# A two-layer hybrid trunk: the decay step ahead of a rotation, a joint opened on 256 columns, a table load moved behind a split, whole tiles two units later

## What is computed

```python
h   = rmsnorm(x) * (1 + scale1) + shift1
# one projection of h in parts: u, q, k, v, z, xbc, dt
A   = pooling_mixer(u)                    # windows 2/4/8/16
B   = differential_attention(q, k, v)     # rotary on the latent q, k; 4 heads
C   = ssd_mixer(conv(xbc), dt, z)         # chunked scan, both directions
x  += gate1 * (out_proj(sum of sigmoid(gates(h)) * branch_proj(A, B, C)))
x  += gate2 * conv_ffn(rmsnorm(x) * (1 + scale2) + shift2)
```

## Time and profile before

| what | value |
|---|---|
| runs | 1292.47, 1293.12, 1292.94 us; median 1292.94 |
| profiled execution | 1292.74 us |
| its span in the profile | 1290.9 us, so 1.84 us lie around it |
| TensorE's granted clock | 0.998 of full speed |
| PE busy | 1272.4 us |
| DVE busy | 1084.3 us |
| ACT busy | 651.0 us |
| POOL busy | 196.6 us |

### The profile page before, as it was taken

How to read it: one execution, slowest core, us unless ns; L and a number is a source line. 1 busy time by engine, 2 the same in 40 slices (tenths; PEclk the granted TensorE clock), 3 DMA queues, 4 the chain that set the end, 5 groups by cost and what they waited for, 6 DMA issues and landing times.

```text
span 1290.9 us, 20336 instructions
## 1 busy us (share of the span) xinstructions
PE 1272.4 (99%) x7704; PEld 1227.6 (95%) x7704; DVE 1084.3 (84%) x1996; ACT 651.0 (50%) x1098; POOL 196.6 (15%) x191
## 2 busy tenths in 40 slices
PE   7999999999999999999999999999999999999997
PEld 5999899999999999999999988999999999999997
DVE  6899978788988999999969998877988799999433
ACT  5633555655565554443374336654455754544432
POOL 0269100002200000001104950000040000000110
PEclk9999999999999999999999999999999999999999
DMA  9566446444533454457735662564445354544441
GB/s 362 201 229 212 148 139 218 167 148 131 164 130 131 133 170 155 147 191 273 234 120 168 227 210 84 178 230 149 137 126 194 93 168 132 166 139 161 152 127 57
DMA packets 60482, 216.26 MB, mean 168 GB/s; under 512 B 7105, under 2 KB 9409, under 8 KB 58849
## 3 DMA queue, kind: packets, MB, share of 16 engines
q1 hardware_dynamic: 56224, 199.38, 46.1%
q0 software_dynamic: 4016, 15.39, 3.8%
q10 hardware_dynamic: 144, 0.20, 0.0%
HBM read 211.17 MB, written 3.77 MB: 166 GB/s over the span
## 4 chain that ended last, share of the span: by engine, by line
PE 87%; DVE 7%; ACT 3%; issue 1%; DMA 1%; SPq 1%; DVEq 0%; ACTq 0%
PE acc L1052 27%; PE acc L1054 26%; PE acc L1053 26%; DVE wl L1827 2%; DVE junk_front L1916 2%; PE mixes L1322 1%; DMA head<-in_whead_dram 1%; PE mixes L1256 1%; ACT th L1452 1%; ACT hh L1441 1%; PE mixes L1226 1%; PE acc L984 0%; PE mixes L1238 0%; ACT cv L1452 0%; PE misc L1342 0%
## 5 line engine op out<-in xcount | busy, mean ns | idle before, releaser
L1052 PE MATMUL acc<-hh,wh 128*128 128x384 f32 x1519 | 516.2, 340 | 0.5 <-DVE wl L1827 0.2
L1054 PE MATMUL acc<-hh,wl 128*128 128x384 f32 x1519 | 507.8, 334 | 0.0
L1053 PE MATMUL acc<-hl,wh 128*128 128x384 f32 x1519 | 507.7, 334 | 0.0
L1827 DVE TENSOR_TENSOR wl<-raw,wh 128x1024 fp32r<-128x1024 f32 (+1 forms) x276 | 343.3, 1245 | 62.4 <-ACT wh L1416 60.5
L1416 ACT ACTIVATE wh<-raw 128x1024 fp32r<-128x1024 f32 (+1 forms) x276 | 286.7, 1041 | 138.2 <-PE acc L1054 135.8
L1052 PEld LDWEIGHTS acc<-hh,wh 128*128 128x128 f32 x1519 | 285.2, 188 | 8.8 <-issue 3.4
L1053 PEld LDWEIGHTS acc<-hl,wh 128*128 128x128 f32 x1519 | 285.3, 188 | 1.5
L1054 PEld LDWEIGHTS acc<-hh,wl 128*128 128x128 f32 x1519 | 285.1, 188 | 0.0
L2008 DVE SCALAR_TENSOR_TENSOR cv<-acc,prm,cv 128x1 f32<-128x1 f32 (+1 forms) x416 | 153.5, 410 | 7.9 <-ACT cv L1579 0.8
L1052 PE MATMUL acc<-ah,wh 128*128 128x384 f32 x352 | 117.7, 334 | 0.0
L1054 PE MATMUL acc<-ah,wl 128*128 128x384 f32 x352 | 117.6, 334 | 0.0
(11 more groups left out here) (324 smaller groups left out, 1687.0 us busy)
## 6 DMA issues: line engine op xcount, KB each, us to landing
raw<-in_wstream_dram SPq DMA_DIRECT2D x248, 512.0 KB, 3.6
rawm<-in_wstream_dram SPq DMA_DIRECT2D x80, 512.0 KB, 4.3
raw<-in_wstream_dram SPq DMA_DIRECT2D x32, 448.0 KB, 3.5
head<-in_whead_dram SPq DMA_DIRECT2D x8, 1024.0 KB, 15.7
rowf<-runs_dram POOLq DMA_DIRECT2D x12, 256.0 KB, 4.2
rowb<-runs_dram POOLq DMA_DIRECT2D x12, 256.0 KB, 4.8
crow_late<-in_cvec_rows_dram POOLq DMA_DIRECT2D x2, 1024.0 KB, 6.3
crow<-in_cvec_rows_dram POOLq DMA_DIRECT2D x2, 1024.0 KB, 5.4
```

Of the source, the lines that this page charges most:

```text
L1052: mm(out, sh, mhi, start=start, stop=False)
L1053: mm(out, sh, mlo, start=False, stop=False)
L1054: return mm(out, sl, mhi, start=False, stop=stop)
L1827: tt(wl[:, s, 0:n], raw[:, raw_slot(u), 0:n], wh[:, s, 0:n].bitcast(F32), ALU.subtract).then_inc(lo_done, 1)
```

## The change

It has four parts.

1. **Joint.** In `joint`, the six high matmuls of the first activation tile, of 384 columns, become six of 256 columns, released by a new semaphore `first_half` after ACT's first piece, and six of 128 columns, released by `h_hi` as before. This holds for three joints, 18 matmuls more in all.
2. **Table load.** The load of the tanh table goes from the end of `norm` to a place behind the split of unit 3's weight, for all but the first norm.
3. **Decay step.** In `mixers_b` the block for slot 2 stands ahead of the rotation.
4. **Whole tiles.** They stand behind units 5 to 12.

```diff
-WHOLE = range(JOINT, JOINT + KT)
+WHOLE = range(JOINT + 2, JOINT + 2 + KT)
...
+                for v, (a0, a1) in enumerate(SEGS):
+                    if v == 0:
+                        pe.wait_ge(first_half, nth + 1)
+                    else:
+                        pe.wait_ge(h_hi, count(l, NSPLIT, split0))
+                    for i in range(JOINT):
+                        w1, w2 = weights(i, 0)
+                        mm(banks[i][:, a0:a1], w1, hh[:, 0, a0:a1], start=(v == 0), stop=False)
+                        mm(banks[i][:, a0:a1], w2, hh[:, 0, a0:a1], start=False, stop=False)
                 for k in range(KT - 2):
-                    pe.wait_ge(h_hi, count(l, NSPLIT, split0 + k))
-                    for i in range(JOINT):
-                        w1, w2 = weights(i, k)
-                        mm(banks[i][:, 0:T], w1, hh[:, k, :], start=(k == 0), stop=False)
-                        mm(banks[i][:, 0:T], w2, hh[:, k, :], start=False, stop=False)
+                    if k:
+                        pe.wait_ge(h_hi, count(l, NSPLIT, split0 + k))
+                        for i in range(JOINT):
+                            w1, w2 = weights(i, k)
+                            mm(banks[i][:, 0:T], w1, hh[:, k, :], start=False, stop=False)
+                            mm(banks[i][:, 0:T], w2, hh[:, k, :], start=False, stop=False)
...
                             last = af(hh[:, j, a0:a1], b[:, a0:a1], ACT.Identity, bias=mod[:, shift0 + j, v:v + 1])
+                            if j == 0 and v == 0:
+                                last.then_inc(first_half, 1)
                         last.then_inc(h_hi, 1)
                     else:
                         affine(b, scale, shift0, j)
                         high(l, None, hh[:, j, :], b)
-                act.preload_act_table_set(TANH_EXP)
...
                     if joint_place(u) == 0:
                         ahead(l, u)
+                        if l or u:
+                            act.preload_act_table_set(TANH_EXP)
...
-                if s in ROTATE_SLOTS:
-                    i = ROTATE_SLOTS.index(s)
-                    rotate(l, (QQ, KK)[i % 2], i // 2 + 1)
                 if s == 2:
...
                     last.then_inc(ada_done, 1)
+                if s in ROTATE_SLOTS:
+                    i = ROTATE_SLOTS.index(s)
+                    rotate(l, (QQ, KK)[i % 2], i // 2 + 1)
```

More of the change, by code:

```diff
@@ L562, in build @@
         h_hi = sem("h_hi")
+        first_half = sem("first_half")
         h_lo = sem("h_lo")
@@ L1128, in joint @@
             def joint(l, u0, split0):
-                kind = UNITS[u0][0]
+                kind, nth = UNITS[u0][0], norm_number(l, u0 > 0)
                 banks = []
```

## The result

The changed kernel takes 1294.24 us (median of 20 runs, 1293.69 to 1296.05); the kernel before, in 20 runs beside them, 1292.47. The ratio is 1.0014, with a 95% interval of 1.0008 to 1.0021: 1.8 us slower, less than the 2.6 us that I had set as the bound of what can be told, but clear of zero. The prediction of no change at 1292.8 lies 1.4 us too low, the time lies inside the range, and the sign was not forecast.

A forecast was written before the change was run, and what follows sets the result against it. PE, busy 99% of the span, bounds the kernel, so only its stalls count. −1.24 − 0.24 + 0.5 − 0.35 + 1.0 + 0.15 = −0.18 gave about 1292.8 us, no measurable change; 8-in-10 range 1291.0 to 1295.6.

The forecast's parts named there:

- The decay step: Slot 2, both layers: PE's 0.46 us wait for `adt` before the cumulative products goes, −0.62 each, −1.24 us in sum.
- The table load: Three joints: stall behind goes, −0.35 kept in layer 1's first projection; both up-projections +0.5 each, +1.0 in sum.
- The chain without PE in it: Up-projections: DVE and ACT wait on each other from the taps to the low part; no slack, PE 0.5 us late.
- Rival C: Up-projections: ACT pauses as long again behind the moved load, both 1.3 us later, +2.6, 1295.4 us; chance 0.03.
- The joint: Three openings: PE could start 0.29 us earlier but needs `hl` anyway, gain 0; narrow matmuls cost +0.05 each, +0.15.
- rival B: Three openings: 128-column products charged as two passes, 0.22 us each, +2.1 instead of +0.15, 1294.8 us; chance 0.22.
- The whole tiles: Layer 1's convolution stall goes, −0.24 us; POOL's pooling passes delay DVE before the first transpositions, +0.5 (0 to +2.0).
- the slack at the transpositions: First transpositions: DVE ends `pr` at 144.81, PE begins at 145.48; with 0.11 handover, 0.56 us of slack.
- The idle time of 0.7: DVE's 0.7 us idle in the window POOL newly fills; the reason for taking the middle lag, 0.8 us.
- The 19%: Share of DVE's time lost beside POOL: a weight's low part takes 1506 ns, alone 1.22 us; applied to 8.3 us.
- Rival A: Pooling lag and up-projection taps are absorbed: −2.5 us, 1290.4, or 1289.5 with the openings; chance 0.15, beyond 0.2% in 0.06.
- D: Slot 2: the decay step's new place does nothing, PE already stands at the queue's order; 1294.0 us; chance 0.02.

## Why the prediction was right in most of its parts and wrong in its sum

**The decay step** was forecast at −1.24 and gave −1.24 in the trace and −1.3 alone. The wait, the engine it ended on, and the claim that the later rotation is not missed all held.

**The table load** was forecast at −0.35 + 1.0 = +0.65; the trace has +0.7 and the part alone +0.5. The chain without PE in it, the 0.5 us by which the taps come later and the unit at which that comes out were right. On the drain that the Trainium skill's page "ScalarE: Activation LUTs" counts in "What ACT_TABLE_LOAD costs", the new place shows what the old did: the load of 390.91 ends at 392.19 and the product begins at 392.20. Ahead of the load there is no pause either, since the activation before it ends at 390.89. Rival C falls with that.

**The joint** was forecast at +0.15 and gave 0. The low products wait for `hl` as said, and the narrow step is the 0.11 that was taken and not the 0.22 of rival B, so each 128-column matmul with rounded operands is a single instruction (PE's count grows by 18, not more).

**The whole tiles** are the step that failed, and in it one term: "DVE could lag between 0 and 8.3 × 0.19 = 1.6 us at 142.8. I take the middle, 0.8". The lag is 1.87, above the bound too. That turned a forecast of no change (−0.18) into a loss of 1.8. The mechanism (POOL's passes stretch DVE's work, and PE waits for it) and the slack at the transpositions (0.56) were right; with 1.87 in place of 0.8 the same working gives 1.87 − 0.56 = 1.3 per layer, 2.6 in both, which is what PE lost. The idle time of 0.7, a wait for ACT, was used up as I had expected; the stretch that it was taken from was too small, 2.7 us (2.5 + 0.2 above) and not 1.6 at most. The 19% is a mean over passes that stretch a long DVE instruction by up to 0.84 us and passes that don't stretch it at all. And I put it on the 8.3 us alone that had been free of POOL: there DVE lost only 0.8, and most of the rest was lost earlier, where sums of the pooling mixer had come to lie beside long instructions. That the time still fell inside the stated range is luck: the room at its upper end was there for rival B, and not for this term. I also looked for the lag at the transpositions alone; it comes out first at the scores, by way of ACT. That changes the place and not the sum, since what PE loses at the first it does not lose again.

**Rival A** (nothing replaces the waits) fell on the same rows. So did **D**. Of the forecast's sum of −0.18, +2.2 was missing in that one term, and the rest was right to within 0.3.

## What to carry to other kernels

An engine off the critical path still has a clock that others run by: work of POOL that moves by 8 us without changing its length can cost PE more than 1 us in each layer, if a busy DVE comes late by it. Such a price is worked out pass by pass, from how much longer DVE's own instructions take beside each kind of pass than alone, over all of the stretch in which DVE has no pause, and not from a mean share in the window that the move newly fills; idle time is taken off that whole stretch. A fixed cost such as a table load is moved behind everything that the next engine waits for, not only behind the first; and parts that share a lag don't add up, since one can hide what another costs.

## What was not expected of the hardware

Single DVE instructions of 1.22 us took up to 2.07 beside POOL (one line's instructions, after):

```profile
L1930 DVE SCALAR_TENSOR_TENSOR junk_front<-rawm,crow x56: 1210/1408/2067, 74.6 to 767.3; 128x1024 f32<-128x1024 f32 x56
```

The median of this line in the changed kernel is 1408 ns, where it is 1220 with POOL's passes left out (the whole tiles, which stay, still stretch some). It takes POOL: between 75 and 800 us, in ten of the traces, no `junk_front` or `wl` of 1024 columns took over 1.23 us without an instruction of POOL beside it. The page "SBUF — State Buffer" of the Trainium skill says in "Who interferes with whom" that a DVE instruction with two SBUF inputs contends with a GpSimd instruction that reads SBUF, which agrees: these instructions have two. Which side loses differs here from pass to pass: DVE beside the window sums (2.06 us), POOL beside the edge correction (1.18 where 0.20 is its shortest). What decides it was not tested. A matmul of 128 columns that follows one of 256 began 0.06 us after the one before, and the next ones 0.11 (380.21, 380.27, 380.38 above): it is not known here what sets the 0.11.
